# Modulation blocks in pairs on half the TensorE columns, x ahead of the weights, expert weights laid out in 16 KB pieces

## The reference, cut to what matters

```
mod_ctx = silu(c_ctx) @ w_ada + b_ada        # w_ada is 1024 x 6144; one vector for the context tokens
mod_lat = silu(c)     @ w_ada + b_ada        # one for the latent tokens
shift1, scale1, gate1, shift2, scale2, gate2 = split(mod, 6)
h  = rms_norm(x, norm1_g) * (1 + scale1) + shift1
z  = h @ w_in                                # 1024 x 8192: convolution, q, k, v, two gates
...                                          # convolution, differential attention, merge, w_o
x  = x + gate1 * (mixed @ w_o)
h2 = rms_norm(x, norm2_g) * (1 + scale2) + shift2
for e in range(16):                          # top 1 of 4 groups, top 2 of its 4 experts
    he = silu(t @ w1[e]) * (t @ w3[e])       # 1024 x 512 each
    y += combine[:, e] * (he @ w2[e])        # 512 x 1024
```

## Time and profile before

| | us |
|---|---|
| median of three runs | 1475.68 |
| the profiled execution | 1474.83 |
| its span, first to last instruction | 1473.1 |
| TensorE busy | 1378.2 (94%) |
| VectorE busy | 389.9 (26%) |
| ScalarE busy | 228.0 (15%) |
| GpSimd busy | 143.0 (10%) |
| mean granted TensorE clock | 0.982 of full |

### The profile page before, as it was taken

How to read it: one execution, slowest core, us unless ns; L and a number is a source line. 1 busy time by engine, 2 the same in 40 slices (tenths; PEclk the granted TensorE clock), 3 DMA queues, 4 the chain that set the end, 5 groups by cost and what they waited for, 6 DMA issues and landing times.

```text
span 1473.1 us, 11868 instructions
## 1 busy us (share of the span) xinstructions
PE 1378.2 (94%) x4780; PEld 709.2 (48%) x4781; DVE 389.9 (26%) x783; ACT 228.0 (15%) x449; POOL 143.0 (10%) x149
## 2 busy tenths in 40 slices
PE   5999988899988899999999999999969999999995
PEld 1444345444255455555555555554544444444442
DVE  0321057321067711211000000004661232232232
ACT  3211045211055100000200000002111011011010
POOL 0132000132000000000000000000010222222221
PEclk9999999999999999999999999999979999999998
DMA  9511430011520001303100510053167988988961
GB/s 349 210 58 65 171 122 1 15 57 65 205 88 1 0 1 57 115 0 114 58 1 0 200 57 0 0 190 153 58 230 277 362 325 331 367 328 331 342 244 55
DMA packets 93346, 206.38 MB, mean 140 GB/s; under 512 B 8880, under 2 KB 9200, under 8 KB 93296
## 3 DMA queue, kind: packets, MB, share of 16 engines
q1 hardware_dynamic: 80864, 184.16, 34.1%
q0 software_dynamic: 12000, 20.48, 3.8%
q10 hardware_dynamic: 432, 1.05, 0.2%
HBM read 205.61 MB, written 23.10 MB: 155 GB/s over the span
## 4 chain that ended last, share of the span: by engine, by line
PE 87%; DVE 5%; DMA 3%; ACT 3%; issue 1%; SPq 0%; POOL 0%; POOLq 0%; DVEq 0%; ACTq 0%
PE psum L1283 33%; PE psum L1388 14%; PE psum L1195 14%; PE psum L1406 7%; PE psum L1165 5%; PE psum L1310 4%; PE psum L1267 3%; PE psum L1244 2%; PE psum L1260 2%; DMA arena<-rows_scratch 1%; DMA x<-in_x_prompt 1%; DVE arena L824 1%; PE psum L1379 1%; DVE softmax_stats L850 1%; ACT arena L644 1%
## 5 line engine op out<-in xcount | busy, mean ns | idle before, releaser
L1283 PE MATMUL psum<-arena,weight_ring 128*128 128x128 f32 (+1 forms) x1792 | 487.6, 435 | 1.7 <-ACT arena L678 1.7
L1283 PEld LDWEIGHTS psum<-arena,weight_ring 128*128 128x128 f32 x1792 | 271.4, 192 | 217.8 <-issue 217.8
L1388 PE MATMUL psum<-weight_ring,arena 128*128 128x512 f32 x512 | 224.3, 596 | 0.0
L1195 PE MATMUL psum<-weight_ring,arena 128*128 128x512 f32 x480 | 209.8, 593 | 2.0 <-ACT arena L589 1.5
L1388 PEld LDWEIGHTS psum<-weight_ring,arena 128*128 128x128 f32 x512 | 97.0, 192 | 115.9 <-issue 115.9
L563 ACT ACTIVATE arena<-psum 128x512 f32<-128x512 f32 (+4 forms) x84 | 49.6, 597 | 594.8 <-PE psum L1283 431.3
L1195 PEld LDWEIGHTS psum<-weight_ring,arena 128*128 128x128 f32 x480 | 89.5, 190 | 106.6 <-issue 104.3
L1406 PE MATMUL psum<-arena 128*128 128x512 f32 x256 | 112.6, 593 | 0.7 <-ACT arena L713 0.7
L1165 PE MATMUL psum<-weight_ring,silu_c 128*2 128x512 f32 x192 | 86.2, 604 | 16.2 <-DMA weight_ring<-in_w_ada 16.2
L492 POOL DMA_INDIRECT arena<-h_scratch,slot_tokens x16 | 15.4, 961 | 747.5 <-DVE slot_tokens L1054 742.9
L1310 PE MATMUL psum<-weight_ring,arena 128*128 128x512 f32 x160 | 73.7, 610 | 3.9 <-DVE arena L939 2.1
(11 more groups left out here) (200 smaller groups left out, 800.8 us busy)
## 6 DMA issues: line engine op xcount, KB each, us to landing
weight_ring<-in_w SPq DMA_DIRECT2D x32, 2048.0 KB, 12.7
weight_ring<-in_w_in SPq DMA_DIRECT2D x16, 2048.0 KB, 8.2
arena<-in_w SPq DMA_DIRECT2D x16, 2048.0 KB, 12.1
weight_ring<-in_w_ada SPq DMA_DIRECT2D x12, 2048.0 KB, 8.4
weight_ring<-in_w_conv_out SPq DMA_DIRECT2D x2, 2048.0 KB, 7.7
weight_ring<-in_w_attn_out SPq DMA_DIRECT2D x2, 2048.0 KB, 7.8
arena<-rows_scratch SPq DMA_DIRECT2D x8, 512.0 KB, 7.6
weight_ring<-in_w_o SPq DMA_DIRECT2D x2, 2048.0 KB, 7.7
```

The source lines that it names most:

```text
L1195: last = mm(ps[:, 0:512], hT[:, k, P * i:P * (i + 1)], w[:, k, :], start=(k == 0), stop=(k == KT - 1))
L1283: last = mm(ps[:, lo:hi], w[:, k, P * (n % 4):P * (n % 4 + 1)], src[:, k, lo:hi], start=(k == 0), stop=(k == KT - 1))
L1388: last = mm(psum[:, 1024 + 512 * j:1536 + 512 * j], xgT[:, t, :], w[:, t, :], start=(t == 0), stop=(t == KT - 1))
```

## The change

Three edits, which touch different stages.

1. **Pairs.** The 12 chunks of `w_ada` are made in six jobs of two chunks: (0,2), (1,3), (4,5), (6,7), (8,9), (10,11). The stationary operand is widened from 2 to 64 columns, the other 62 zero (`lanes_c`, filled by a DVE memset and an ACT copy). The first chunk of a pair writes PSUM partitions 0 to 63, the second 64 to 127, with matmuls that alternate between the two. `adaT` is now four full 128x128 transposes, and DVE adds the bias in two instructions a pair.
2. **Start.** SP loads x first, then pairs 0 and 1 in halves of four row tiles. PE takes each half when it lands, and the `xT` jobs stand between the pairs. Pair 0 holds chunk 0 of shift1 and chunk 0 of scale1, so half of the channels get scale and shift before pair 1 is in. Squares and scaling of x are split: three tiles on ACT, two on DVE.
3. **Experts.** Row `8 p + k` (`4 p + k` in the down weights) lies on partition p: each partition gets one run of 16 KB. To match, the transposes of tokens and hidden rows take every 8th (4th) column of their source.

```
+ACT_TILES = 3
+LANE = 64
+ADA_PAIRS = [(0, 2), (1, 3), (4, 5), (6, 7), (8, 9), (10, 11)]
...
-    names = [("ada", n) for n in range(4)]
+    names = [("ada", n) for pair in ADA_PAIRS[0:2] for n in pair]
...
+    jobs = [("ada", 0, "act"), xT(1), ("adaT", 0, "dve"), xT(0), xT(3), ("ada", 1, "act"), xT(2), ("adaT", 1, "dve")]
+    jobs += [xT(k) for k in (5, 4, 7, 6)]
...
-        jobs += ada(4 + 4 * g)
+        jobs += [("ada", 2 + 2 * g, "act"), ("ada", 3 + 2 * g, "act"), ("adaT", 2 + 2 * g, "dve"), ("adaT", 3 + 2 * g, "dve")]
...
         def up_src(w, e):
-            return w[e].rearrange("(k p) n -> p k n", p=P)
+            return w[e].rearrange("(p k) n -> p k n", p=P)
         def down_src(e):
-            return io["w2"][e].rearrange("(k p) n -> p k n", p=P)
+            return io["w2"][e].rearrange("(p k) n -> p k n", p=P)
...
-            load_chunk(0)
             sp.dma_start(x_sb[:, 0:4 * D].rearrange("p (i n) -> p i n", i=4), io["x_sample"].rearrange("(i p) n -> p i n", p=P)).then_inc(s_x, 16)
             sp.dma_start(x_sb[:, 4 * D:], io["x_prompt"]).then_inc(s_x, 16)
-            for n in range(1, 4):
-                load_chunk(n)
+            for p in range(2):
+                for half in range(2):
+                    for c in range(2):
+                        n = 2 * p + c
+                        part = slot[n].rearrange("p (k n) -> p k n", k=KT)[:, 4 * half:4 * half + 4, :]
+                        src = chunk_src(CHUNK_LIST[n])[:, 4 * half:4 * half + 4, :]
+                        sp.dma_start(part, src).then_inc(s_w[n] if half else s_early[p], 16)
...
+            dve.wait_ge(s_x, 32)
+            for i in range(ACT_TILES, NT):
+                x_i = x_sb[:, D * i:D * (i + 1)]
+                link(V.tensor_tensor(xn[:, i, :], x_i, x_i, mult))
+                V.reduce_sum(stat[:, i:i + 1], xn[:, i, :], axis=AX).then_inc(s_xss, 1)
...
-                for k in range(KT):
-                    last = mm(ps[0:2, 0:512], sc[:, k, :], w[:, k, :], start=(k == 0), stop=(k == KT - 1))
+            def ada_part(p, ps, half, srcs):
+                for k in range(4 * half, 4 * half + 4):
+                    for lane, w in enumerate(srcs):
+                        last = mm(ps[LANE * lane:LANE * (lane + 1), 0:512], lanes_c[:, k, :], w[:, k, :], start=(k == 0), stop=(k == KT - 1))
+                return last
...
-                    last = tr(ps[:, 2 * t:2 * t + 2], ada_rows[n % 2][:, P * t:P * (t + 1)], ident[0:2, 0:2])
+                    last = tr(ps[:, P * t:P * (t + 1)], ada_rows[p % 2][:, P * t:P * (t + 1)], ident[:, :])
...
-            pe.wait_ge(s_xn, NT)
+            early_ada(0)
+            x_T(1)
+            ada_T(0)
+            x_T(0)
+            x_T(3)
+            early_ada(1)
+            x_T(2)
+            ada_T(1)
+            for k in (5, 4, 7, 6):
+                x_T(k)
...
-                ada_all(4 + 4 * g)
+                for p in (2 + 2 * g, 3 + 2 * g):
+                    ada(p)
+                for p in (2 + 2 * g, 3 + 2 * g):
+                    ada_T(p)
...
-                    last = tr(psum[:, P * t:P * (t + 1)], xg[b][:, P * t:P * (t + 1)], ident[:, :])
+                    every = xg[b].rearrange("p (q k) -> p k q", k=KT)
+                    last = tr(psum[:, P * t:P * (t + 1)], every[:, t, :], ident[:, :])
```

More of the change, by code:

```diff
@@ L62, in psum_jobs, with xT @@
 def psum_jobs():
[L64 to L73, removed]
+    def xT(k):
+        return ("xT", k, "dve" if k % 2 == 0 else "act")
+    jobs = [("ada", 0, "act"), xT(1), ("adaT", 0, "dve"), xT(0), xT(3), ("ada", 1, "act"), xT(2), ("adaT", 1, "dve")]
+    jobs += [xT(k) for k in (5, 4, 7, 6)]
     for g in range(GROUPS):
@@ L120, in last_use @@
     if kind == "ada":
-        return INDEX[name]
+        return INDEX[("ada", next(p for p, pair in enumerate(ADA_PAIRS) if n in pair))]
     if kind == "o":
@@ L578, in _ @@
             act.wait_ge(s_xrs, 1)
-            for i in range(NT):
+            for i in range(ACT_TILES):
                 A(xn[:, i, :], x_sb[:, D * i:D * (i + 1)], ACT.Copy, scale=stat[:, 2 * NT + i:2 * NT + i + 1]).then_inc(s_xn, 1)
[L581 to L591, removed]
+            ada_copy(0)
+            xT_copy(1)
+            xT_copy(3)
+            ada_copy(1)
+            xT_copy(5)
+            xT_copy(7)
             act.wait_ge(s_lamx, 1)
@@ L631, in _ @@
                     v_copy(i)
-                for n in range(4):
-                    ada_copy(4 + 4 * g + n)
+                for n in range(2):
+                    ada_copy(2 + 2 * g + n)
                 emptied(act, INDEX[("v", NT * g + CTX)])
@@ L756, in _ @@
-            for n in range(4):
-                ada_copy(n)
-            emptied(dve, INDEX[("adaT", 3)])
-            V.scalar_tensor_tensor(out=a1[:, :].rearrange("p (k v) -> p k v", v=2), in0=mod[:, 16:32].rearrange("p (k v) -> p k v", v=2),
-                                   scalar=1.0, in1=col("g1").unsqueeze(2).to_broadcast([P, KT, 2]), op0=add, op1=mult).then_inc(s_mod1, 1)
-            dve.wait_ge(s_mod1, 1)
-            for k in range(0, KT, 2):
+            dve.wait_ge(s_xrs, 1)
+            for i in range(ACT_TILES, NT):
+                V.tensor_scalar(xn[:, i, :], x_sb[:, D * i:D * (i + 1)], stat[:, 2 * NT + i:2 * NT + i + 1], None, mult).then_inc(s_xn, 1)
@@ new lines, in ada_copy @@
+            def ada_copy(p):
+                job_done(dve, "adaT", p)
+                made = job_psum("adaT", p)[:, 0:512].rearrange("p (t l v) -> p l t v", t=4, v=2)
+                for lane, n in enumerate(ADA_PAIRS[p]):
+                    last = V.tensor_tensor(mod[:, 8 * n:8 * n + 8].rearrange("p (n v) -> p n v", v=2), made[:, LANE // 2 * lane],
+                                           col("b_ada")[:, 4 * n:4 * n + 4].unsqueeze(2).to_broadcast([P, 4, 2]), add)
+                last.then_inc(s_emptied["dve"], 1)
@@ new lines, in first_scale @@
+            def first_scale(p):
+                ada_copy(p)
+                emptied(dve, INDEX[("adaT", p)])
+                V.scalar_tensor_tensor(out=a1[:, 8 * p:8 * p + 8].rearrange("p (k v) -> p k v", v=2),
+                                       in0=mod[:, 16 + 8 * p:24 + 8 * p].rearrange("p (k v) -> p k v", v=2), scalar=1.0,
+                                       in1=col("g1")[:, 4 * p:4 * p + 4].unsqueeze(2).to_broadcast([P, 4, 2]), op0=add,
+                                       op1=mult).then_inc(s_mod1, 1)
+                dve.wait_ge(s_mod1, p + 1)
@@ L764, in _, with xT_copy @@
+            def xT_copy(k):
                 job_done(dve, "xT", k)
@@ L852, in _ @@
                         mix(n - 1)
-            emptied(dve, INDEX[("adaT", 11)])
+            emptied(dve, INDEX[("adaT", 5)])
             m6 = mod[:, :].rearrange("p (s k v) -> p s v k", s=6, v=2)
```

79 lines of the change are left out of this document (48 added, 31 removed).

## The result

| | us |
|---|---|
| before, median of 4 runs beside it | 1474.88 |
| after, median of 4 runs (1434.74 to 1441.85) | 1435.28 |
| ratio, 95% interval | 0.9735 [0.9696, 0.9773] |
| the profiled execution, its span | 1434.74, 1433.0 |
| mean granted TensorE clock | 0.986 (before 0.982) |

The change takes 39.6 us off. 19.7 were forecast, so the direction is right and the forecast has only half of the size; the time lies at the low edge of the range, near rival 1 (strided loads are free, 1440).

What follows compares the result with a forecast made beforehand. TensorE's own work was taken as the bound (busy 1378.2 of 1473.1 us). 1474.83 - 24.6 - 10.3 + 15.5 - 0.5 = 1454.9; with the run median 0.85 above the profiled execution, forecast 1456 (chance 0.43, own range 1450 to 1461), range 1435 to 1469.

Steps and rivals of the forecast that it cites:

- rival 1: Expert transposes: strided weight loads are free, all else as forecast, total 1440 us; chance 0.30.
- The start: Up to the first projection: x first and halved pairs start it at 44.5 instead of 54.8, -10.3 us.
- The slow first records: First 16 matmul records at the start: PE begins at half pace after idling, adding 2.1 us.
- The pairs: Two-chunk modulation jobs: both column groups overlap, 17 x 0.43 = 7.3 us a pair; bounds 7.0 and 14.0.
- the rule: Pairs on PE: records start in program order, once their half is free and the previous record has started; gives 7.3 us.
- The late blocks: Between v and the scores, groups 0 and 1: scores start 12.3 us earlier in each, -24.6 us together.
- The expert transposes: Expert stage: strided weight loads add 0.106 us per transpose, 146 paid, +15.5 us; bounds 0 and 20.
- 16 KB pieces: Expert weight loads: nothing in the steady stage, a shorter PE wait at the first expert, -0.5 us.
- rival 5: Expert stage: long weight pieces crowd out the gathers, +31 us, total 1487; chance 0.04.
- rival 2: Pairs: column groups take turns, 14.0 us a pair, and strides cost as forecast, total 1494 us; chance 0.11.
- rival 3: Pairs and expert transposes: column groups take turns and strided loads are free, total 1478, about no change; chance 0.07.
- rival 4: Pairs: weight loads come late, about 0.11 us at 16 places, a pair of 9.0, total 1463 us; chance 0.05.

Runs made afterwards that it cites:

- experiment 8: Changed kernel with x loaded behind the first halves of pair 0 instead of ahead of them: 1437.95 us, ratio to the kernel before 0.9758.
- experiment 9: Changed kernel with x first, then pairs 0 and 1 loaded in whole chunks, PE waiting for both chunks of a pair: 1442.38 us, ratio 0.9782.
- experiment 3: Changed kernel with, inside each pair, four matmuls of one half of the array before four of the other: 1444.46 us, ratio 0.9785; a pair 8.4 us.
- experiment 11: Changed kernel plus unused work at its end: 16-column matmuls at steps 1, 2, 4, 8 (0.142, 0.213, 0.233, 0.238 us), column and row groups in blocks.
- the bench: Changed kernel plus unused series behind the last hidden transpose: transposes at steps 1, 2, 4, 8, 32 took 0.109, 0.120, 0.120, 0.112, 0.112 us.
- experiment 1: Changed kernel with the expert edit undone (weights laid out as before, contiguous transposes): 1435.24 us, ratio to the kernel before 0.9735.
- experiment 2: Kernel before with the expert edit alone (16 KB pieces, strided transposes): 1474.25 us against 1474.48, ratio 1.0003.
- experiment 12: Changed kernel with four groups of 32 columns, both late pairs still after the v projection: 1433.26 us, ratio 0.9714.

## Why the prediction was half right

- **The start, -10.3: right (-10.4).** x landed at 13.8 (14.6 forecast), and the chain runs as forecast through pair 1's landing. The slow first records cost 2.0 us (9.07 for a pair against 7.09), 2.1 forecast. The closeness is in part luck: that landing came at 35.4 and not 36.1, and from it to the projection it took 9.0 us and not 8.4. Experiments 8 and 9 give two parts, the order of x 2.0 (against x between the halves, not against the order before) and the halves 4.3; that the remaining 4 belong to the pairs is a subtraction and no run shows it.
- **The pairs, 7.3 us each: right (7.10).** The halves alternate record by record here, two loads a step, so the rule and the array's looser order come to the same. The page of the Trainium skill "TensorE: Matmul & The Clock Gate", Part 3, says that loads overlap only where the row group differs; here both groups have the same rows, and 32 loads hid in 7.10 us. By that rule the pair would have taken more. Experiments 3 and 11 show that my own rule was too strict for other orders.
- **The late blocks, -24.6: right to 1.1 (-25.7).** (192.78 - 180.4 is 12.4 and not 12.3; it changes nothing.) The new wait was 1.27 us, 1.0 forecast; copies, `adaT` and bias took 1.79, 1.9 forecast.
- **The expert transposes, +15.5: wrong.** This is the failed step: "If the weight path of PE gets one strided element in 1.68 ns too, it takes 0.215 us and sets the pace: +0.106." Measured: +0.003 to +0.011 per transpose in the bench, 0.04 us an expert in the kernel, 0.6 in all. The weight loads of the token transposes did grow in the records; grouped by line, before and then after:

```profile
L1379 PEld LDWEIGHTS psum<-ident,arena 128*128 128x128 f32 x128 | 15.6, 146 | 12.8 <-issue 12.8
```

```profile
L1428 PEld LDWEIGHTS psum<-ident,arena 128*128 128x128 f32 x128 | 17.2, 192 | 12.1 <-issue 12.1
```

The longer record is no slower pace. Eight transposes still took 0.88 us, since each load starts while the one before it is under way, and contiguous loads of ordinary matmuls have records of 190 ns too (the q, k and v projections). A strided element cost a transpose 0.87 to 0.94 ns (0.112 and 0.120 us for 128), where I had put DVE's 1.68. The rule of the Trainium skill in "SBUF — State Buffer", Door 1 (lines of 16 bytes, two hits per line), holds for DVE (419 against 318 ns) and for the streaming operand, which doubles at a step of 4; it does not tell what transposes do. The step of four f32 that the page calls free cost the streaming operand 0.90 us against 0.43, and DVE 1048 ns against 686.
- **16 KB pieces, -0.5: right in kind.** They give nothing measurable (experiments 1 and 2): the term was put at 0.5 and is not there. No gather was crowded out (rival 5).
- **With +0.6 in place of +15.5 the sum is 1441.** Of the 6 us left, 1.1 are in the late blocks and 4.4 are the granted clock in stages that did not change. No step of mine could have told the latter; it is an error of a few us in any such sum. Why the clock fell in some executions and not in others stays open.

Of the rivals, 2 to 5 are refuted by the chain (pair 7.10, no wait of PE in the steady expert stage); rival 1 is what happened. I gave it 0.30 against 0.43, on the word of another engine's row. All of PE's rows that I had were contiguous, and the term lay between honest bounds (0 and 20); which end to take was a guess. The time ended only 0.3 us inside the range.

## What to carry to other kernels

Matrix-vector work on the f32 array fills one column group: put independent vectors, or parts of one contraction, into groups of 64 or 32 columns, alternate between them record by record, and the time falls by 2 and by 4 (here from 14.0 us for two chunks to 7.1 and 3.57). Move such work to where its weights have long been loaded, since a bared wait of some 5 us cost 2.0 to 2.5 us more in clock (experiments 8 and 12). A price measured on one engine is no value for another's, nor for another operand of the same engine: a bench of 24 instructions measures it. Read the granted clock of each series of a bench before comparing them; experiment 11 would otherwise give a cost of 1.67 times that is nearly all clock.

## What the runs showed of the hardware

- Four column groups with different weights and different streams do 64 f32 records in 7.07 us, where 16 of one group take 7.03: 4.0 times.
- PE runs three to four records of another group ahead of waiting ones, for column and for row groups: two groups in blocks of 8 matmuls took 12.29 and 12.39 us, where strict order gives 13.3.
- A step in the streaming operand costs 5% at 2 f32 (0.45 us against 0.43) and doubles the time at 4 and 8 (0.90, 0.93). In a transpose's stationary operand it costs at most 10% (0.120 us against 0.109, full clock). In that of a matmul whose load sets the pace it costs 0, 9 and 12% at steps 2, 4 and 8, at a clock of 0.50; the full clock was not measured.
- Matmuls of 16 columns, back to back and without a gap, went from a granted clock of 1.00 to 0.50, and a record from 0.112 to 0.213 us.
- A wait of 1.27 us left the granted clock at 1.00 (the pair took 7.09); waits of 4.55 and 5.33 us were followed by 0.50. After 2.19 us the next 4 us read once 0.76 (a mean of both levels) and once 1.00, at the same place of the program.
